# An order written by a planner: state-space steps, gate projection and residual row sums moved in a one-core two-block kernel

## The reference, cut to what matters

```python
h = rms_norm(x, g_pre_mix) * (1.0 + sc_m) + sh_m
u, f, q, k, v = split(h @ w_in)             # widths 384, 256, 384, 128, 128
y_ssm = s5_mixer(u, ...)                    # two-way scan, 24 groups, gelu, then y * sigmoid(y @ w_glu)
y_fft = fourier_mixer(f, w_fft)             # real part of a 2-D FFT, then a 64x64 product per head
y_att = window_attention(q, k, v, sink)     # 6 heads, blocks of 128, window 128
y = concat([y_ssm, y_fft, y_att]) @ w_out
x = x + gt_m * rms_norm(y, g_post_mix)      # mod = c @ w_ada + b_ada gives sh, sc, gt
h = rms_norm(x, g_pre_ffn) * (1.0 + sc_f) + sh_f     # then the MLP with w_up and w_down
```

## Time and profile before

| | |
|---|---|
| median of 3 runs | 2755.02 us (2753.72 to 2757.47) |
| profiled execution, its own time | 2753.72 us |
| its span, first to last instruction | 2751.9 us |
| TensorE busy | 2637.7 us, 96% of the span |
| VectorE busy | 1465.6 us, 53% |
| GpSimd busy | 1091.4 us, 40% |
| ScalarE busy | 1029.3 us, 37% |

### The profile page before, as it was taken

One profiled execution on the slowest core, in us unless ns is written; L12 is line 12 of the kernel. 1 busy time (PEld: TensorE's weight loads), 2 busy tenths in 40 slices (PEclk: granted clock), 3 DMA queues, 4 the chain that ended last, 5 costly groups with the idle time before them and its releaser, 6 DMA issues.

```text
span 2751.9 us, 31627 instructions
## 1 busy us (share of the span) xinstructions
PE 2637.7 (96%) x12542; PEld 2080.4 (76%) x12542; DVE 1465.6 (53%) x1881; ACT 1029.3 (37%) x1600; POOL 1091.4 (40%) x605
## 2 busy tenths in 40 slices
PE   6889989999999999999999999999999999999997
PEld 2657757777888788877777788888788788888885
DVE  5646658797777722276766422433457655322225
ACT  4413655455444511345454321211354434312112
POOL 1322114256656544442211142322353655534443
PEclk8999999999999999999999999999999999999998
DMA  6453247321222343241123122111324233433322
GB/s 247 178 146 101 78 173 285 113 81 66 81 84 83 112 146 126 84 145 59 54 68 109 54 88 67 58 48 48 137 91 153 77 115 104 149 118 128 115 77 85
DMA packets 109619, 297.92 MB, mean 108 GB/s; under 512 B 13344, under 2 KB 28192, under 8 KB 109472
## 3 DMA queue, kind: packets, MB, share of 16 engines
q1 hardware_dynamic: 102592, 275.36, 29.4%
q10 hardware_dynamic: 3456, 10.73, 1.0%
q0 software_dynamic: 3424, 9.81, 0.9%
HBM read 233.09 MB, written 62.76 MB: 108 GB/s over the span
## 4 chain that ended last, share of the span: by engine, by line
PE 71%; DVE 5%; ACT 1%; issue 1%; POOL 1%; DMA 1%; POOLq 0%; SPq 0%; DVEq 0%; ACTq 0%
PE ps L1698 16%; PE ps L1700 15%; PE ps L1699 15%; PE ps L1732 5%; PE ps L1734 5%; PE ps L1733 5%; PE pc L1732 1%; PE pc L1734 1%; PE pc L1733 1%; PE pss L2026 1%; PE pc L2078 1%; PE pc L2080 1%; PE pc L2079 1%; POOL whl L3448 1%; DVE pad L2104 0%
## 5 line engine op out<-in xcount | busy, mean ns | idle before, releaser
L3448 POOL TENSOR_TENSOR whl<-wraw,whl 128x1024 fp32r<-128x1024 f32 (+2 forms) x309 | 648.0, 2102 | 1242.0 <-ACT whl L2918 1241.8
L1698 PE MATMUL ps<-act,whl 128*128 128x512 f32 x1824 | 735.5, 403 | 34.7 <-DVE act L2098 9.2
L1699 PE MATMUL ps<-act,whl 128*128 128x512 f32 x1824 | 718.0, 394 | 0.0
L1700 PE MATMUL ps<-act,whl 128*128 128x512 f32 x1824 | 717.5, 393 | 0.0
L1698 PEld LDWEIGHTS ps<-act,whl 128*128 128x128 f32 x1824 | 344.9, 189 | 134.9 <-issue 43.3
L2918 ACT ACTIVATE whl<-wraw 128x1024 fp32r<-128x1024 f32 (+2 forms) x309 | 268.1, 869 | 461.9 <-PE ps L1700 372.6
L1700 PEld LDWEIGHTS ps<-act,whl 128*128 128x128 f32 x1824 | 344.9, 189 | 76.9
L1699 PEld LDWEIGHTS ps<-act,whl 128*128 128x128 f32 x1824 | 345.3, 189 | 75.7 <-issue 4.1
L2098 DVE TENSOR_TENSOR y<-y,ps 128x512 f32<-128x512 f32 x176 | 120.9, 687 | 365.6 <-PE ps L1700 365.4
L1698 PE MATMUL ps<-hid,whl 128*128 128x512 f32 x544 | 216.8, 399 | 4.4 <-DVE y L2502 4.3
L1700 PE MATMUL ps<-hid,whl 128*128 128x512 f32 x544 | 214.4, 394 | 0.0
(11 more groups left out here) (402 smaller groups left out, 4206.1 us busy)
## 6 DMA issues: line engine op xcount, KB each, us to landing
wraw<-in_w_in SPq DMA_DIRECT2D x63, 512.0 KB, 3.4
wraw<-in_f1u SPq DMA_DIRECT2D x72, 256.0 KB, 2.8
wraw<-in_f2d SPq DMA_DIRECT2D x36, 512.0 KB, 3.4
wraw<-in_w_out SPq DMA_DIRECT2D x32, 512.0 KB, 3.4
x<-in_w_ada SPq DMA_DIRECT2D x32, 512.0 KB, 7.2
hid<-hscr SPq DMA_DIRECT2D x29, 512.0 KB, 6.6
xs<-y SPq DMA_DIRECT2D x24, 512.0 KB, 6.3
wraw<-in_f2u SPq DMA_DIRECT2D x48, 256.0 KB, 3.3
```

The source lines that it names most:

```text
L1698: pe.matmul(PSB[g.bank][:, :], hi, x_hi, start=e == 0, stop=False)
L1699: pe.matmul(PSB[g.bank][:, :], hi, x_lo, start=False, stop=False)
L1700: m = pe.matmul(PSB[g.bank][:, :], lo, x_hi, start=False, stop=e == len(ks) - 1)
L3448: return g_.tensor_tensor(out, a, b, op)
```

## The change

It reorders the plan, and moves or drops two waits:

- `ssm`: `ssm_y(b-1)` and `ssm_out(b-1)` come directly after `ssm_rot(b, 1)`. Before, they came 4.0 planner microseconds later, after `ssm_scan(b, 1)`. `ssm_x(b+1)` comes before the scans. Before, it came after them.
- `glu`: the first product is due 3.0 after `glu_gelu` and no longer 9.5.
- `residual`: for half 1 of s = 1 and 2, the start is due 2.7 after and no longer 6.0.
- `fft_out` (VectorE): the wait for `fft_mid` stands ahead of the first copy and no longer ahead of the last one.
- `mod_c` (SyncE): it no longer waits for the load of uT (`d_yl`).

```diff
@@ def ssm()
             yield 1.5
             p.put("ssm_rot", b, 1)
-            yield 2.5
-            p.put("ssm_scan", b, 1)
-            yield 1.5
             if b:
                 p.pe(2.7, "ssm_y", b - 1)
                 p.put("ssm_out", b - 1)
-            yield 0.5
+            yield 2.5
+            if b < 5:
+                p.pe(1.8, "ssm_x", b + 1)
+            p.put("ssm_scan", b, 1)
+            yield 2.0
             p.put("ssm_scan", b, 0)
             yield 2.0
-            if b < 5:
-                p.pe(1.8, "ssm_x", b + 1)
             p.put("ssm_back", b, 0)
@@
         p.put("glu_gelu")
-        yield 9.5
+        yield 3.0
@@ def residual(s, half, final=False)
-        yield 6.0 if half and s in (1, 2) else 2.7
+        yield 2.7
@@ VectorE, def fft_out(pr)
                 w.wait_ge(*done("fft", "s", 7))
+                w.wait_ge(*done("fft", "mid"))
                 v.tensor_copy(st[:, 0:512], Pb[:, :]).then_inc(*mark("fftD", "a", pr))
...
-                w.wait_ge(*done("fft", "mid"))
                 v.tensor_copy(st[:, 512:513], PSS[:, 0, pr:pr + 1]).then_inc(*mark("fftD", "st", pr))
@@ SyncE, def mod_c()
                 w.wait_ge(*done("ssm", "y", 5))
-                w.wait_ge(*done("d_yl", 2))
```

## The result

The changed kernel takes 2772.25 us (median of 5 runs, 2767.45 to 2777.39). The kernel before takes 2755.02 in the same comparison. The ratio is 1.0058, with a 95% interval of 1.0042 to 1.0075. That is 16 us slower (11.6 to 20.7), on the forecast's side. The time lies inside the wide range (2751 to 2775), but 8 us above the forecast of 2764 and 2 us above the forecast's own range (2758 to 2770).

A forecast was written before the change was run, and what follows sets the result against it. TensorE was taken to bound the state-space and attention stretch (busy 181.75 of 196 us). Terms +9.5 + 2.1 - 6.8 + 2.0 + 2.6 = +9.4 on 2755.0 gave 2764 us, own range 2758 to 2770, wide range 2751 to 2775.

The forecast's parts named there:

- wide range: Whole kernel: the range that leaves 0.2 out, 2751 to 2775 us.
- the forecast's own range: Whole kernel: 2758 to 2770 us around the forecast of 2764, which had chance 0.48.
- the signs that I named: TensorE idle at `ssm_y` (1 to 4 us), after Fourier sums (4 to 5), at `r_rows` (4 to 5.5); gelu behind table load.
- Part 1: Order in `ssm`: TensorE stalls at `ssm_y` until "rot", net +9.5 us, ends 0 and +15.
- part 2: `fft_out`: VectorE starts only when `fft_mid` is done, so TensorE starts 2.1 us later and nothing hides it.
- Stands at `ssm_y`: TensorE's stalls in batches 1 to 5: 2.9, 1.2, 2, 1.3 and 3.9 us, plus 0.7 at `ssm_x(2)`, sum 12.0.
- Clock: TensorE in `ssm`: 1.6 us lost per long idle time, three new ones adding 4.8, two present waits' share going.
- Part 3: Gate: gelu starts 5.7 us earlier, a later unit 8.9 earlier; 6.8 us of gain kept, ends 3 and 9.
- Part 4: Residual, half 1: TensorE stands at `r_rows` 5.5 us in stage 1; +2.0 and +2.6 us for the two stages.
- The faster one: Rival: no stalls at `ssm_y` since Cb comes sooner, earlier gate wins, 2748 us; chance 0.17.
- The gate's gain is lost: Rival: VectorE or w_ada rows hold `apply`, only some 2 of 6.8 us kept, part 1 at upper end, 2774; chance 0.15.
- the two present waits: TensorE's 2.37 and 1.70 us waits for a small VectorE result in the kernel before; they go, saving 7.3 with clock.

The follow-up runs named there:

- run 5: Changed kernel without the reloads of Cb (all batches use batch 0's): 0.9998 against the kernel before, -0.6 us (-3.3 to 2.5).
- run 9: Changed kernel with Cb reloaded sooner, behind its last read and ahead of the eight stores of `ssm_out`: 1.002 against the kernel before, +5.5 us.
- run 12: Kernel before with the new `ssm` order, gate edits, sooner Cb reload and both `ssm_rot` halves together at the first's place: 2745.99 us, ratio 0.9959, -11.3 us.
- Run 7: Changed kernel with the old order in `ssm` put back: 1.0027 against the kernel before, +7.4 us (4.7 to 10.5).
- run 1: Kernel before with the new order in `ssm` alone: ratio 1.003 (1.002 to 1.0039), +8.3 us (5.5 to 10.7).
- run 10: Changed kernel without reloads of Cb and with both `ssm_rot` halves together at the second's place: 1.0007 against the kernel before, +1.9 us.

## Why the prediction was right, point by point

The direction holds, and each part has the sign that I gave it. The size doesn't quite: even by the ratio, 2755 + 16 = 2771 is just past the forecast's own range. Of the signs that I named, `ssm_y` stood in batches 1 to 5, the wait behind the Fourier sums was 4.65 us, and gelu came directly behind its table load (395.48 + 1.28 = 396.76, start 396.77). One failed: `r_rows` of half 1 stood 3.96 and 3.09 us, where I had 4 to 5.5 for both stages.

**Part 1, the order in `ssm`: the mechanism holds, the size was too small, and one cause was wrong.** I said +9.5 with an upper end of +15. Up to the attention's end the changed kernel loses 18.1. Of these 2.2 are the longer wait of part 2 (4.65 less 2.45), so part 1 is +15.9, just past its upper end; in the run with the order alone it is +13.4. By terms:

- Stands at `ssm_y`, batches 1 to 5: said 2.9, 1.2, 2, 1.3, 3.9; measured 2.96, 3.31, 3.40, 0.36, 3.98. The mis-sized terms are batches 2 and 3, 3.5 us together. For batch 2 I let the reload go 4 us sooner. It went at 244.68, against 245.13 before. Its condition, H2 of batch 1, was met at 242.83, 2.4 us later than before, and SyncE was still busy: the eight issues of Tb took 4.88 us instead of 3.62, and the stores behind them ended at 244.07. And TensorE was there at 249.05.
- `ssm_x(2)` behind ScalarE's copy: said 0.7, measured 0.78.
- Batch 5 has the right number for the wrong reason. That is luck. I took VectorE to be held by Cb. Runs 5 and 9 show 3.98 and 3.97 us with no reload and with a sooner one, and run 12 shows that the attention step between the halves held it. VectorE's timeline of the kernel before already has that step between the halves, behind the landing of Cb:

```profile
343.78 0.68 DVE L2098 TENSOR_TENSOR Mt<-pc,Cb 128x512 f32<-128x512 f32 x1
344.38 0.61 DVE L2390 CUSTOM_DVE_ANT_0 sc<-pss,dist,par 128x384 f32<-128x384 f32 x1
...
346.01 0.67 DVE L2098 TENSOR_TENSOR Mt<-pc,Cb 128x512 f32<-128x512 f32 x1
```

- New waits that I had not counted, for qT and pt: 1.7 us in all (0.78 before 346.54, 0.56 before 388.78, and some tenths at the old ones).
- Clock: I said 1.6 net. The idle time up to the attention's end is 14.6 us more than before. The rest of the 18.1, 3.5 us, is the same work done at a lower mean clock. With the order alone it is 1.1.

**Part 2, `fft_out`:** said +2.1. The stand is 2.20 us longer both in the changed kernel and with the edit alone. Alone it is worth 0.8 (-1.4 to 3.3), so "nothing hides it" is neither shown nor refuted: the trace keeps 2.5 us of delay for the next 150 us, and what is gone behind that is the clock's.

**Part 3, the gate:** said -6.8 net, with 8.9 gross. ScalarE evicts the first w_out tile at 425.81, 33.7 us behind the attention's end, and before at 416.89, 42.6 behind it: 8.9 less. At `r_rows` 7.6 are left. By the traces 5.9 come with the order (uT back sooner) and 1.8 with the two edits, the latter no more than a cell's error.

**Part 4, the residual:** said +4.6 (2.0 and 2.6). Measured alone +4.4, and in the changed kernel's trace +2.7 and some +3. The stands are 3.96 and 3.09 us, where I had 5.5 and 4. In stage 1 the last unit ahead of `r_rows` starts at 508.53, 4.87 us before the sum ends (513.40). Before, that distance belongs to the unit at 497.90, one later (1.3 us) than the one that I counted from. So the stands are 1.5 and 0.9 us shorter than I said, and that the sum still comes out at +4.4 is partly luck. What fills the difference isn't broken down: the eight matmuls take 0.9 us more in either stage of the changed kernel, but with the edit alone those of stage 2 take only 0.1 more (1.05 us behind the same 3.09).

**The rivals.** The faster one needed that no stands appear. They do, in five batches. "The gate's gain is lost" named the nearer time, 2774 against 2764, and half of its reason is there (part 1 at its upper end), but the gain of the gate was kept. By the instants, the miss of 16.1 - 9.4 = 6.7 us is 6.4 in part 1, 0.1 in part 2 and 1.0 in part 4, less 0.8 in the gate.

**Landing and clock.** The Trainium skill, page "DMA: Bandwidth & Descriptors", section "Anatomy of one DMA — SWDGE (gpsimd) path", gives 2.0 us plus bytes over 436 GB/s for a transfer that GpSimd issues. That would be an estimate of 3.2 us for the 512 KB of Cb, but SyncE issues Cb, and the page gives no such sum for that path. The changed kernel's trace says 4.0 to 5.0 with a median of 4.2, and that is the number to use. The Trainium skill, page "TensorE: Matmul & The Clock Gate", section "What's actually happening", says that idleness lowers the clock and activity frees it. The trace agrees for these: behind stands of 3.4 to 4.0 us at `ssm_y`, the windows show 0.50 and 0.52 in the changed kernel and 0.59 and 0.71 in the run with the order alone.

**What stays open.** The single parts sum to +11 by their times, the whole to +16. Interval by interval this can be chance. In the traces 3.4 us of it lies ahead of the attention's end (18.1 - 13.4 - 1.3), and only 0.4 of that is idle time, the rest work at the lower clock. But one trace of each is no proof, and the one with the order alone was the fastest of its run. Run 7, meant for this, did not decide it.

## What to carry to other kernels

In a written-out order, a step moved up on one in-order engine has to be checked against the other engine's order too: what stands between the producer's halves, and whether that waits for the engine that is about to wait. Write down the times of the reload chain (last read, issue, landing, first use) before shortening the plan around it. In this kernel a reload that goes sooner and a yield moved behind the second of two steps turned a loss of 8 us into a gain of 11 (2.5 of it the gate edits'). And compare traces from instant to instant, since spans carry 5 us of difference from before the change.

## What the runs showed of the hardware that I had not expected

**A small VectorE operation held up by GpSimd.** The step on 128x4 numbers usually takes 0.16 us. In batch 5 it took 1.55 to 1.57 in six traces (the changed kernel's and those of runs 1, 5, 9, 10 and 12), and each time it ended 0.01 or 0.02 us after a GpSimd operation that had begun before it. In the changed kernel, VectorE and then GpSimd:

```profile
348.32 1.56 DVE L2103 SCALAR_TENSOR_TENSOR small<-small,par 128x4 f32<-128x4 f32 x1
```

```profile
347.51 2.35 POOL L3447 TENSOR_TENSOR whl<-wraw,whl 128x1024 fp32r<-128x1024 f32 x1
```

348.32 + 1.56 = 349.88, and 347.51 + 2.35 = 349.86. This is 1.4 us of the loop in batch 5, where it stands ahead of "rot". The step on the score ahead of it, which reads one tile from PSUM and one from SBUF, kept its 0.48 us beside the same GpSimd operation (it started at 347.79). The Trainium skill, page "SBUF — State Buffer", section "SBUF: two separate sides", says that a VectorE operation with two SBUF inputs and a GpSimd one that reads SBUF exclude each other for the whole instruction. The trace agrees.

**The clock after a stand is not a fixed price.** In the changed kernel the first two matmuls behind 3.31 us of idle time run at full speed (0.46 us) and slow ones follow 1.0 us later. Behind 3.40 us they are slow at once (0.77). In run 9 they are slow behind only 2.22 us, by its timeline and its window (clock 0.59):

```profile
277.57 0.77 PE L1836 MATMUL pc<-U,Tb 128*128 128x128 f32 x2 [2.22 <-DVE Hb L2097]
```

```profile
277.50:281.50 4.00, 3.93 (x21) 3.96 (x22) 0.65 (x1) 0.00 (x0) 0.00 (x0) 0.59 0.02 4
```

Behind 2.96 us, in the changed kernel's batch 1, no slow matmul follows at all. With the order alone, 3.23 us are followed by a window at full clock. So 1.6 us for each stand is no price that one can rely on. Net of the two present waits I had 1.6 in all, and the traces show 3.5 in the changed kernel and 1.1 with the order alone.
